# Gate/up products of a fused fp32 transformer pair by seven half-size block products in place of eight

## The reference

```python
h = rmsnorm_2(x, g_pre_ffn[l]) * (1.0 + sc_f) + sh_f
f = (jax.nn.silu(h @ w_gate[l]) * (h @ w_up[l])) @ w_down[l]
x = x + gt_f * rmsnorm_2(f, g_post_ffn[l])
```

## Time and profile before

| | |
|---|---|
| three runs | 3204.05, 3206.47, 3208.24 us (median 3206.47) |
| profiled execution | span 3201.8 us from first to last instruction; its records give no other time of its own |
| TensorE | 3156.7 us busy, 14744 matmuls |
| VectorE, ScalarE, GpSimd | 1723.7, 916.3, 268.9 us busy |
| granted TensorE clock | 0.994 of 2.4 GHz on average |
| data moved | 455.83 MB, 142 GB/s |

### The profile page before, as it was taken

One profiled execution on the slowest core, in us unless ns is written; L12 is line 12 of the kernel. 1 busy time (PEld: TensorE's weight loads), 2 busy tenths in 40 slices (PEclk: granted clock), 3 DMA queues, 4 the chain that ended last, 5 costly groups with the idle time before them and its releaser, 6 DMA issues.

```text
span 3201.8 us, 38265 instructions
## 1 busy us (share of the span) xinstructions
PE 3156.7 (99%) x14744; PEld 2603.3 (81%) x14744; DVE 1723.7 (54%) x2260; ACT 916.3 (29%) x1124; POOL 268.9 (8%) x414
## 2 busy tenths in 40 slices
PE   8999999999999999999998999999999999999998
PEld 7888877888878888888777888888888888888887
DVE  6666665868874445556788643333333333323354
ACT  5333343223233333444522221111121121121213
POOL 1111100111100000000013220000000000000013
PEclk9999999999999999999998999999999999999999
DMA  5444455766742222222564642322322223222354
GB/s 185 142 132 133 127 187 215 289 255 230 259 190 79 84 87 79 80 79 79 225 251 169 240 133 92 111 93 100 110 92 101 102 98 105 98 98 102 124 179 163
DMA packets 93449, 455.83 MB, mean 142 GB/s; under 512 B 19744, under 2 KB 20016, under 8 KB 56112
## 3 DMA queue, kind: packets, MB, share of 16 engines
q1 hardware_dynamic: 51776, 298.08, 26.4%
q0 software_dynamic: 37696, 128.52, 11.2%
q10 hardware_dynamic: 3888, 28.03, 2.3%
HBM read 421.81 MB, written 26.22 MB: 140 GB/s over the span
## 4 chain that ended last, share of the span: by engine, by line
PE 96%; DVE 3%; DMA 0%; ACT 0%; DVEq 0%; issue 0%; SPq 0%; ACTq 0%
PE PS L1076 24%; PE PS L1078 24%; PE PS L1077 24%; PE PS L1478 5%; PE PS L1477 5%; PE PS L1476 5%; PE PS L1345 1%; PE PS L1372 1%; PE PS L1129 1%; PE PS L1130 1%; PE PS L1131 1%; PE PS L1360 1%; PE PS L1242 0%; PE PS L1201 0%; DVE WL L1523 0%; PE PS L1224 0%
## 5 line engine op out<-in xcount | busy, mean ns | idle before, releaser
L1076 PE MATMUL PS<-XH,WH 128*128 128x512 f32 x3312 | 1298.0, 392 | 5.8 <-DVE WL L1523 2.8
L1078 PE MATMUL PS<-XH,WL 128*128 128x512 f32 x3312 | 1289.0, 389 | 0.0
L1077 PE MATMUL PS<-XL,WH 128*128 128x512 f32 x3312 | 1288.8, 389 | 0.0
L1523 DVE TENSOR_TENSOR WL<-RAW,WH 128x2048 fp32r<-128x2048 f32 x266 | 609.5, 2292 | 498.8 <-ACT WH L680 498.7
L680 ACT ACTIVATE WH<-RAW 128x2048 fp32r<-128x2048 f32 x266 | 509.0, 1914 | 1242.8 <-PE PS L1078 875.4
L1076 PEld LDWEIGHTS PS<-XH,WH 128*128 128x128 f32 x3312 | 621.7, 188 | 145.8 <-issue 13.5
L1078 PEld LDWEIGHTS PS<-XH,WL 128*128 128x128 f32 x3312 | 621.7, 188 | 130.1
L1077 PEld LDWEIGHTS PS<-XL,WH 128*128 128x128 f32 x3312 | 621.8, 188 | 129.6 <-issue 2.2
L1476 PE MATMUL PS<-WH,FH 128*128 128x512 f32 x704 | 273.9, 389 | 0.0
L1477 PE MATMUL PS<-WL,FH 128*128 128x512 f32 x704 | 273.9, 389 | 0.0
L1478 PE MATMUL PS<-WH,FL 128*128 128x512 f32 x704 | 273.9, 389 | 0.0
(11 more groups left out here) (320 smaller groups left out, 2299.9 us busy)
## 6 DMA issues: line engine op xcount, KB each, us to landing
RAW<-w_units_dram SPq DMA_DIRECT2D x268, 1024.0 KB, 4.8
ADA<-w_ada_dram POOLq DMA_DIRECT2D x192, 512.0 KB, 5.5
spill_dram<-SIG POOLq DMA_DIRECT2D x24, 256.0 KB, 2.3
BB<-x_t_dram ACTq DMA_DIRECT2D x1, 4096.0 KB, 15.8
x_dram<-RES ACTq DMA_DIRECT2D x1, 4096.0 KB, 14.9
BB<-x_dram ACTq DMA_DIRECT2D x4, 1024.0 KB, 7.9
x_dram<-BB ACTq DMA_DIRECT2D x4, 1024.0 KB, 5.1
X3T<-x3t_dram ACTq DMA_DIRECT2D x4, 1024.0 KB, 4.9
```

What stands on the lines that cost most here:

```text
L1076: pe.matmul(PS[:, bank, :], wh, rh[:, x, :], start=k == 0, stop=False)
L1077: pe.matmul(PS[:, bank, :], wh, rl[:, x, :], start=False, stop=False)
L1078: ins = pe.matmul(PS[:, bank, :], wl, rh[:, x, :], start=False, stop=k == n - 1)
L1523: v.tensor_tensor(WL[:, slot, :], RAW[:, slot, :], f32(WH[:, slot, :]), ALU.subtract)\
```

## The change

Two pairs of gate/up units stay as they are (`PLAIN = 2`). The other 42 pairs (`FAST`) are computed by Strassen's scheme. The pair's weight is a 2 x 2 block matrix, whose rows are the k halves (8 k tiles each) and whose columns are gate and up; the activations are a 2 x 2 block matrix of k halves by token halves (256 tokens). Seven products of half size stand in for eight.

- **TensorE** runs seven products of 8 k tiles x 3 passes with 256 columns for each pair, in half banks, three of them added to what an earlier product left in the bank. It waits for `q_lo` (a split weight block) before each product, and for `copied` or `taken` (a bank that has been read).
- **GpSimd** makes the four sums of weight blocks (128x1024 each) in `SUM3`, `SUM2` and in place in the raw weights. The last one waits until block 3 has been split.
- **ScalarE and VectorE** split seven blocks of 128x1024 a pair into a ring of four slots (`QH`, `QL`), three products ahead. ScalarE copies three half banks to SBUF; VectorE makes four results from half banks and one addition in SBUF; ScalarE takes the silu; VectorE multiplies (128x512, both operands in SBUF) into `FO`.
- **SP** loads a pair of units into one of two buffers (`RAWS`, the second where the modulation chunks lay) and stores each hidden tile to a new tensor in memory.
- **Before the first fast pair** VectorE and ScalarE make four differences of activation blocks, shifted and split, in `TA`, `TB` and `TC`, while TensorE runs the plain pairs.
- **The down product** is a second phase after all pairs: 11 chunks of 16 groups of 12 matmuls of 512 columns, as before. Hidden tiles are read back from memory, four at a time, and split again.
- The modulation chunks and the transposes of the residual move into the down phase (one chunk a unit; one transpose every second unit, each loaded from memory).

The loop that SP, GpSimd, ScalarE, VectorE and TensorE run over the fast pairs has four pairs in its body and 10 turns; two pairs follow it.

The core of the diff (TensorE, GpSimd, the splits and the readers, SP, the seam between the phases):

```diff
+PLAIN = 2
+FAST = FF_TILES - PLAIN
+LOOPED = FAST - 2
...
+Q0, TAKEN0, COPIED0 = 7, 8, 6
+PRODUCTS = 7
+HALF_S = S // 2
+FULL_K = DT // 2
+NEED_SUM = {1: 1, 2: 2, 4: 3, 6: 4}
+NEED_T = {1: 2, 2: 1, 4: 4, 5: 3}
...
+    def weight(s2, j):
+        g, u, h = RAWS[s2][:, 0, :], RAWS[s2][:, 1, :], FULL_K * P
+        return [g[:, 0:h], SUM3[:, :], u[:, 0:h], g[:, h:2 * h], SUM2[:, :], u[:, h:2 * h], g[:, h:2 * h]][j]
...
+            with sp.Fori(0, LOOPED // 4) as i:
+                for e in range(4):
+                    for k in (1, 0):
+                        sp.wait_ge(q_lo, 28 * i + (Q0 + PRODUCTS * e + 7 - k))
+                        sp.dma_start(RAWS[e % 2][:, k, :], w_units[bass.ds(8 * i + (U_FFN + 2 * PLAIN + 2 * e + 4 + k), 1)]
+                                     .rearrange("a p n -> p (a n)")).then_inc(pair_loaded[e % 2], 16)
+                    hidden_saved(4 * i + (e + 1), f_d[bass.ds(4 * i + (e + 1), 1)].rearrange("a p n -> p (a n)"),
+                                 (e + 1) % 2)
...
+            def weight_sums(s, r, n):
+                g, u, h = RAWS[r][:, 0, :], RAWS[r][:, 1, :], FULL_K * P
+                gp.wait_ge(pair_loaded[r], n)
+                gp.wait_ge(q_lo, PRODUCTS * s + (Q0 - PRODUCTS + 2))
+                gp.tensor_tensor(SUM3[:, :], g[:, 0:h], u[:, 0:h], ALU.add).then_inc(sum_ready, 1)
+                gp.drain()
+                gp.tensor_tensor(u[:, 0:h], u[:, 0:h], u[:, h:2 * h], ALU.add).then_inc(sum_ready, 1)
+                gp.drain()
+                gp.wait_ge(f_made, PLAIN)
+                gp.wait_ge(q_lo, PRODUCTS * s + (Q0 - PRODUCTS + 5))
+                gp.tensor_tensor(SUM2[:, :], SUM3[:, :], u[:, h:2 * h], ALU.add).then_inc(sum_ready, 1)
+                gp.drain()
+                gp.wait_ge(q_lo, PRODUCTS * s + (Q0 + 4))
+                gp.tensor_tensor(g[:, h:2 * h], g[:, h:2 * h], SUM2[:, :], ALU.add).then_inc(sum_ready, 1)
...
+            def hi_part(s, s2, j, slot, done):
+                act.wait_ge(q_done, done)
+                if j in NEED_SUM:
+                    act.wait_ge(sum_ready, 4 * s + NEED_SUM[j])
+                act.activation(QH[:, slot, :], weight(s2, j), ACT.Copy).then_inc(q_hi, 1)
...
+            for j in range(FF_CHUNK):
+                hidden_hi(0, j)
+            down_hi(0)
...
+            def fast_pair(s, e):
+                b0 = 4 - 4 * (e % 2)
+                q = PRODUCTS * s + Q0
+                for j in range(PRODUCTS):
+                    slot = (PRODUCTS * e + j) % 4
+                    bank = b0 + (0, 3, 2, 0, 1, 3, 2)[j]
+                    pe.wait_ge(q_lo, q + j + 1)
...
+                    for k in range(FULL_K):
+                        wh, wl = (w[:, slot, k * P:(k + 1) * P] for w in (QH, QL))
+                        x = fast_data(j, k)
+                        y = PS[:, bank, 0:HALF_S]
+                        pe.matmul(y, wh, x[:, 0, :], start=k == 0 and j not in (3, 5, 6), stop=False,
+                                  skip_group_check=True)
+                        pe.matmul(y, wh, x[:, 1, :], start=False, stop=False, skip_group_check=True)
+                        ins = pe.matmul(y, wl, x[:, 0, :], start=False, stop=k == FULL_K - 1, skip_group_check=True)
+                    ins.then_inc(q_done, 1)
+
+            pair(U_FFN, O_FFN, X_FFN)
+            third(U_FFN + 2, O_FFN + 2, 2, 2, X_FFN)
+            unit(U_FFN + 3, 1, O_FFN + 3, [FULL], 3, 4, X_FFN)
+            pe.wait_ge(out_read, READ0 + O_DOWN)
+            with pe.Fori(0, LOOPED // 4) as i:
+                for e in range(4):
+                    fast_pair(4 * i + e, e)
...
+            def lo_part(s, s2, j, slot):
+                v.wait_ge(q_hi, PRODUCTS * s + (j + 1))
+                v.tensor_tensor(QL[:, slot, :], weight(s2, j), f32(QH[:, slot, :]), ALU.subtract).then_inc(q_lo, 1)
+
+            def fast_pair(s, e, saved, more=True):
...
+                for j in range(2, PRODUCTS):
+                    if j + 3 < PRODUCTS:
+                        lo_part(s, s2, j + 3, (PRODUCTS * e + j + 3) % 4)
+                    elif more:
+                        lo_part(s + 1, n2, j - 4, (PRODUCTS * e + j + 3) % 4)
+                    if j == 3:
+                        v.wait_ge(copied, 3 * s + (COPIED0 + 2))
+                        v.wait_ge(q_done, q + 3)
+                        v.tensor_tensor(r, r, bank(2), ALU.subtract).then_inc(taken, 1)
+                    if j == 5:
+                        v.wait_ge(q_done, q + 5)
+                        v.tensor_tensor(staged(ST_V), bank(1), staged(ST_P1), ALU.subtract).then_inc(taken, 1)
+                        v.drain()
+                        v.tensor_tensor(r, r, staged(ST_V), ALU.add)
+                    if j == 6:
+                        v.wait_ge(q_done, q + 6)
+                        v.tensor_tensor(staged(ST_U), bank(3), staged(ST_V), ALU.add).then_inc(taken, 1)
+                if more:
+                    lo_part(s + 1, n2, 3, (PRODUCTS * e + PRODUCTS + 3) % 4)
+                v.wait_ge(q_done, q + 7)
+                v.tensor_tensor(staged(ST_G + 1), bank(2), staged(ST_V), ALU.subtract).then_inc(taken, 1)
+                if more:
+                    lo_part(s + 1, n2, 4, (PRODUCTS * e + PRODUCTS + 4) % 4)
+                v.drain()
+                v.wait_ge(silu_done, s + 1)
+                v.wait_ge(f_saved[e % 2], saved)
+                v.tensor_tensor(in_halves(FO[e % 2][:, :]), staged_pair(1, ST_G), staged_pair(0, ST_U), ALU.mult)\
+                 .then_inc(f_made, 1)
```

More of the change, by code:

```diff
@@ L80 @@
 ADA_OUT2 = [4, 0] + [3, 4, 3] * 4 + [4, 0]
[L81 removed]
+ADA_DOWN = {**{n: ADA_FIRST[4] + n - 4 for n in range(4, 20)}, **{n: ADA_FIRST[5] + n - 22 for n in range(22, 38)}}
+TURN_DOWN = {4 + 2 * t: t for t in range(DT)}
 LAG = 1
@@ L1467, in _ @@
             token_rows(4, 4, 5)
-            def down(slot, bank, b, ks=range(FF_CHUNK)):
-                for k in ks:
-                    first, last = k == 0, k == FF_CHUNK - 1
-                    fh, fl = FH[:, k, b * P:(b + 1) * P], FL[:, k, b * P:(b + 1) * P]
-                    wh, wl = WH[:, slot, k * S:(k + 1) * S], WL[:, slot, k * S:(k + 1) * S]
-                    pe.matmul(PS[:, bank, :], fh, wh, start=first, stop=False, skip_group_check=True)
-                    pe.matmul(PS[:, bank, :], fh, wl, start=False, stop=False, skip_group_check=True)
-                    ins = pe.matmul(PS[:, bank, :], fl, wh, start=False, stop=last, skip_group_check=True)
-                return ins
@@ new lines, in _, with down_lo @@
+            ins.then_inc(t_lo, 1)
+            lo_part(0, 0, 3, 3)
+            lo_part(0, 0, 4, 0)
+            with v.Fori(0, LOOPED // 4) as i:
+                for e in range(4):
+                    fast_pair(4 * i + e, e, 32 * i + 16 * (e // 2 + 1))
+            fast_pair(LOOPED, 0, 8 * LOOPED + 16)
+            fast_pair(LOOPED + 1, 1, 8 * LOOPED + 16, False)
+            def down_lo(n):
+                slot = (n + 1) % 2
+                v.wait_ge(d_hi, n + 1)
+                v.tensor_tensor(WL[:, slot, :], RAW[:, slot, :], f32(WH[:, slot, :]), ALU.subtract).then_inc(d_lo, 1)
```

528 lines of the change are left out of this document (353 added, 175 removed).

## The result

The changed kernel takes **3155.0 us** (median of four runs, 3154.3 to 3157.3), the kernel before 3205.8 in runs on the same chip: a ratio of 0.9845, 95% interval 0.9831 to 0.9859. It is 51 us or 1.6% faster, eight times what a measurement can tell; 3157 was forecast, with a range of 3105 to 3225.

A forecast was written before the change was run, and what follows sets the result against it. TensorE's matmul time, 99% busy, was taken to bound the kernel. From the 3201.8 us span, 69.3 came off for the pairs and 20 went on for seams: 3152.5, with 4.7 to the median 3157 us, range 3105 to 3225.

The forecast's parts named there:

- both bounds: TensorE's time for a fast pair: 19.0 us at 113.3 ns a matmul or 20.2 us at 120.0 ns.
- VectorE's line: Feeding of a fast pair: VectorE's records, held up by GpSimd's sums, need 19.5 to 20.4 us, taken as 20.0.
- The pair: Each of 42 fast pairs takes 20.1 us in place of 21.75, a gain of 69.3 us in all.
- 6 us of slack: In the loop, a low part may start 6 us early; GpSimd's sums eat about 4 us of this per pair.
- short stalls ahead of product 5 or 6: Sign of being right: in each pair TensorE stalls briefly there, until VectorE's low part ends.
- No stall in the loop: Sign of being wrong: TensorE never waits within the fast pairs.
- The exclusion: VectorE operations with two SBUF inputs and GpSimd's sums shut each other out, holding VectorE 9.1 us more a pair.
- The seams: Gaps before the first fast product, 7 us, and before the down product, 8, plus 5 of slowed clock: 20 us.
- TensorE alone as the pace: Rival, 18%: in the pairs the exclusion costs only slack; at 113.3 ns a matmul the time is 3113 us.
- the third rival: 12%: in the loop's VectorE queue, exclusion takes whole records on every operation; pair 21.7 us, time 3224, slower.
- The mildly late engines: Rival, 13%: sums of 2.58 us or handoffs between the engines make the pair 21.0 us, time 3195.
- Waiting for a load of 188 ns: Rival, 4%: short matmuls run slower or wait for their weight load; pair 31.6 us, 413 us lost, time 3640.

The follow-up runs named there:

- half-weights run: The changed kernel with the fast products' matmuls using only 64 of a block's 128 weight columns: 3124.4 us.
- two-pass run: The changed kernel without the third pass of the fast products, 112 instead of 168 matmuls a pair: 3108.9 us.

## Why the prediction was right, and where it was not

- **Matmul time.** "If they are paid per matmul, 120.0": that bound is the measured 119.97 ns. The prediction kept both bounds (19.0 and 20.2) and leaned on VectorE's line to choose. The upper one holds because the 13.3 ns are paid by each matmul, whatever its columns; the half-weights run shows that 5.1 of them hang on the width of the block.
- **The pair.** 20.1 us forecast, 20.16 measured; gain 66.8 us for 69.3. The number holds, its reason only in part. The two lines were seen as level, with VectorE's at 20.0 "about balance"; VectorE's is at 19.1 and TensorE alone paces. At 113.3 ns TensorE would have asked for 19.0 and the pair, by an estimate from the 19.1 of that line, been near 19.1; that 20.1 came out is partly luck, since the line that chose between the bounds was itself 0.9 us too long.
- **The step that failed** is the one that says 6 us of slack would be eaten at a rate of 4 us a pair and "short stalls ahead of product 5 or 6" follow. There are none in 42 pairs. "No stall in the loop" was listed as a sign of being wrong, and of this step it is one. The terms of the line were mis-sized in both directions. Held records were to cost VectorE 4 x (2.43 - 0.15) = 9.1 us on top of 10.4; they cost 6.0 on top of 10.75 (16.8 busy with the sums, 10.75 without), because three sums a pair meet VectorE and the fourth runs while it stands. The 2.3 us a pair that VectorE stands in the ring of silu, copy and high part were not in the sum. So 19.5 to 20.4 against 19.1 is near by two errors. The two-pass run shows that the stalls come once TensorE is faster: ahead of product 5 in 40 pairs, ended by VectorE's low part as described, and ahead of product 6 in 20, ended by VectorE's read of a bank.
- **The exclusion.** A sum at 2.43 us alone: 2.42. Up to 3.5 beside VectorE: 3.40 on average for the first one. Low parts above 1.22: 2.1 for raw blocks, two of five a pair at 3.4. The Trainium skill (SBUF — State Buffer, SBUF: two separate sides) has the other engine fully blocked for the instruction. The trace agrees: held low parts end 1.08 us behind the end of the sum beside them, about what an operation of 1.22 us needs that starts only then.
- **The seams.** 7 and 8 us forecast, 7.25 and 7.59 over a normal spacing measured, at the places and by the queues described, the 2.2 us lost to GpSimd's sum among them (3 were counted). The clock cost 1.7 + 2.1 us, not 5. Together 18.6 for 20.
- **The sum.** 3201.8 - 66.8 + 18.6 = 3153.6 for a span of 3152.8: what is left unexplained is under 1 us. Two errors, 2.5 us in the pairs and 1.4 in the seams, cancelled in part. The 4.7 us from the span to the median were 2.2 here (3155.0 - 3152.8), which makes up most of the 2 us by which 3157 was too long.
- **Rivals.** TensorE alone as the pace was named as a rival, but at 113.3 ns and 3113 us. Its mechanism is what happened, at the other bound's price, where it cannot be told from the forecast by the time. Of the third rival the whole records are real, but only on operations with both inputs in SBUF: a read of a PSUM bank at 1821.85 takes its usual 0.41 us inside a sum of 3.20. And three sums meet VectorE, not four, so the price of 21.7 us a pair did not come. The mildly late engines (21.0) did not happen either. Waiting for a load of 188 ns did not either: loads of 192 ns overlap at 120 ns spacing.

## What to carry to other kernels

Seven products for eight are an eighth less work, but the pair became only 7.3% shorter, since half-size matmuls pay the fixed 13.3 ns twice as often; count such a price before cutting matmuls, and look for passes that can share a weight load again. Where two lines come out level, find the second one by making the first cheaper, as the two-pass run does: that is where the next change will stop. Where VectorE and GpSimd both read SBUF, count how many operations of one meet the other: each can cost a whole operation of the other engine. A gap at a seam moves rather than goes until everything behind it in the queues is early as well, loads included; and an engine at 93% can feed without a stall when its queue is in the order in which others wait for it.
